# First expert routed alone, gathers in four column groups, and w_out read in eights, in a two-block layer

## The reference

```python
h = h + concat(ssd_out, sc_out) @ w_out            # 2048 -> 1024
hn = rmsnorm(h, norm_ffn)
g_idx = argmax(hn @ w_router_group)                # 4 groups
e_logits = einsum("nd,gde->nge", hn, w_router_expert)   # 8 experts in each
top_v, top_i = top_k(e_logits of the chosen group, 2)
gates = softmax(g_logits)[g_idx] * softmax(top_v)
# each token goes to its two experts:
y = (silu(x @ w_gate[e]) * (x @ w_up[e])) @ w_down[e]   # 1024 -> 512 -> 1024
h = h + sum over the two of gates * y
```

## Time and profile before

| | |
|---|---|
| median of 3 runs | 955.83 us (955.31 to 957.48) |
| the profiled execution | 955.47 us, span 953.7 us |
| TensorE busy | 782.6 us, 82% of the span |
| VectorE busy | 465.6 us, 49% |
| ScalarE busy | 318.0 us, 33% |
| GpSimd busy | 99.0 us, 10% |
| HBM read | 284.85 MB, mean 300 GB/s over the span |
| chain that ended last | TensorE 54%, DMA 28%, issue 8%, VectorE 4%, GpSimd 3%, ScalarE 2% |

### The profile page before, as it was taken

One profiled execution on the slowest core, in us unless ns is written; L12 is line 12 of the kernel. 1 busy time (PEld: TensorE's weight loads), 2 busy tenths in 40 slices (PEclk: granted clock), 3 DMA queues, 4 the chain that ended last, 5 costly groups with the idle time before them and its releaser, 6 DMA issues.

```text
span 953.7 us, 15749 instructions
## 1 busy us (share of the span) xinstructions
PE 782.6 (82%) x6548; PEld 601.2 (63%) x6548; DVE 465.6 (49%) x815; ACT 318.0 (33%) x525; POOL 99.0 (10%) x116
## 2 busy tenths in 40 slices
PE   5999999999984764747646566479999999999997
PEld 5988999777643432334423333236888888888885
DVE  6865849547421121201302012024968776766776
ACT  5764346732100000000000000003597554444444
POOL 3019673300000000000000000000000100000000
PEclk9999999999997887777979798779999999999999
DMA  9895243677999999999999999999975455555101
GB/s 318 272 354 177 90 177 145 259 311 294 415 427 428 426 429 426 427 427 429 428 429 427 428 429 427 429 428 388 363 266 178 155 189 201 183 177 177 45 1 45
DMA packets 72534, 286.67 MB, mean 301 GB/s; under 512 B 11882, under 2 KB 38688, under 8 KB 59936
## 3 DMA queue, kind: packets, MB, share of 16 engines
q1 hardware_dynamic: 71876, 284.81, 75.9%
q10 hardware_dynamic: 604, 1.10, 0.3%
HBM read 284.85 MB, written 1.05 MB: 300 GB/s over the span
## 4 chain that ended last, share of the span: by engine, by line
PE 54%; DMA 28%; issue 8%; DVE 4%; POOL 3%; ACT 2%; SPq 1%; POOLq 0%; DVEq 0%; ACTq 0%
DMA pair_d<-in_w_up_dram 22%; PE bank L664 11%; PE bank L613 11%; PE bank L629 9%; PE bank L2264 5%; PE bank L626 4%; PE bank L2288 4%; PE bank L641 4%; DMA ring<-in_w_in_dram 3%; DMA down_b<-in_w_down_dram 3%; PE bank L2230 1%; PE bank L2238 1%; PE bank L2095 1%; POOL seg_r L946 1%; ACT w_hi L583 1%
## 5 line engine op out<-in xcount | busy, mean ns | idle before, releaser
L593 DVE TENSOR_TENSOR w_lo<-ring,w_hi 128x1024 fp32r<-128x1024 f32 x135 | 174.7, 1294 | 101.9 <-ACT w_hi L583 101.5
L583 ACT ACTIVATE w_hi<-ring 128x1024 fp32r<-128x1024 f32 x136 | 144.2, 1060 | 178.3 <-PE bank L629 64.1
L613 PE MATMUL bank<-act_p,w_hi 128*128 128x256 f32 x736 | 137.7, 288 | 3.1 <-issue 2.0
L1776 DVE COPY y_e<-bank 32x256 f32<-32x256 f32 x64 | 27.2, 424 | 222.5 <-PE bank L2288 222.1
L629 PE MATMUL bank<-act_p,w_hi 128*128 128x512 f32 x344 | 119.3, 397 | 0.0
L613 PEld LDWEIGHTS bank<-act_p,w_hi 128*128 128x128 f32 x736 | 115.3, 192 | 6.0 <-issue 3.9
L1226 ACT ACTIVATE y_e<-bank 32x256 f32<-32x256 f32 x64 | 23.9, 374 | 256.7 <-PE bank L2288 256.4
L613 PE MATMUL bank<-act_p,w_lo 128*128 128x256 f32 x368 | 104.3, 283 | 0.0
L2288 PE MATMUL bank<-down_b,h_t 128*32 128x256 f32 x480 | 40.3, 493 | 74.6 <-issue 64.1
L664 PE MATMUL bank<-w_hi,act_q 128*128 128x512 f32 x288 | 90.6, 396 | 1.4 <-issue 0.8
L2264 PE MATMUL bank<-ring,moe 128*32 128x256 f32 x1472 | 84.0, 380 | 7.1 <-DVE moe L1739 6.7
(11 more groups left out here) (409 smaller groups left out, 1058.5 us busy)
## 6 DMA issues: line engine op xcount, KB each, us to landing
ring<-in_w_up_dram SPq DMA_DIRECT2D x24, 2048.0 KB, 34.6
ring<-in_w_gate_dram SPq DMA_DIRECT2D x23, 2048.0 KB, 30.2
down_a<-in_w_down_dram SPq DMA_DIRECT2D x15, 2048.0 KB, 25.9
down_b<-in_w_down_dram SPq DMA_DIRECT2D x15, 2048.0 KB, 25.8
ring<-in_w_in_dram SPq DMA_DIRECT2D x14, 2048.0 KB, 17.4
ring<-in_w_ffn_in_dram SPq DMA_DIRECT2D x22, 1024.0 KB, 7.6
pair_d<-in_w_gate_dram SPq DMA_DIRECT2D x8, 2048.0 KB, 30.0
pair_d<-in_w_up_dram SPq DMA_DIRECT2D x8, 2048.0 KB, 34.4
```

The lines of the kernel that those rows point to most:

```text
L583: nc.scalar.activation(parts(w_hi, g, view), view, ACT.Copy).then_inc(split_hi, 1)
L593: engine.tensor_tensor(parts(w_lo, g, view), view, h, ALU.subtract).then_inc(split_lo, 1)
L613: mm = nc.tensor.matmul(dst, parts(wt, g, grans[g][1])[:, k, :], a[:, x_part, k, :], start=(k == 0 and i == 0), stop=(k == KC - 1 and i == 2))
L1776: ins = nc.vector.tensor_copy(out_rows(e, j), down_rows(j))
```

## The change

- **w_out in eights.** The granules of w_out are read through a view that puts column c*128 + q where 8q + c was: both splits read words 32 bytes apart, in runs of 128, and write them side by side. The product then has the order of `res`, and `add_res` adds plain halves.
- **Token copy.** GpSimd copies the tokens into `res` after its masks and after granule 0 (`gran_used` 1) and no longer ahead of them.
- **First expert alone.** VectorE first finds only whether a token goes to expert 0: at most one expert of group 0 has a larger logit, and group 0 has the top group logit. Three matmuls of one column give its ranks, and its one-hot follows. The rest of the routing comes behind, with `keep_alone(0)` in its midst; the full ranks (`ranks`) come behind expert 0's gate and up on TensorE.
- **Gathers in column groups.** `gather_alone` takes the one-hot's 32 columns as weights and moves `res` through, 256 features to each of four column groups. The result has slots on partitions; `keep_alone` transposes it in blocks of 32x32 into the tile `gated` and multiplies it with the gain into `x_t`. Experts 0 to 3 have a gather each: 0 ahead of its gate, 1 ahead of its gate, 2 and 3 behind expert 1's gate and up. `gated` is scratch here, and so the combination matrix is built after the fourth.
- **Fillers** are half as wide and stand in more places.

```diff
@@ -225,9 +225,10 @@
-    def row_grans(u, gains):
+    def row_grans(u, gains, eights=False):
         for j, gain in enumerate(gains):
-            grans.append((u, whole(u)[:, j * GR:(j + 1) * GR], gain))
+            view = whole(u)[:, j * GR:(j + 1) * GR]
+            grans.append((u, view.rearrange("p (q c) -> p c q", c=KC) if eights else view, gain))
@@ -250,7 +251,7 @@
         row_grans(rows_unit(w["w_out"], ks[0], 4),
-                  [pcol("sc_norm", k - 8) if k >= 8 else pcol("ssd_norm", k) for k in ks])
+                  [pcol("sc_norm", k - 8) if k >= 8 else pcol("ssd_norm", k) for k in ks], True)
@@ -677,9 +678,9 @@
         for at, (b, half) in enumerate(BY_BLOCK):
-            r = natural(b, 64 * half, 64 * half + 64)
+            r = res[:, b, half * 512:(half + 1) * 512]
             piece_ready(dve, n, at, g)
-            ins = nc.vector.tensor_tensor(r, r, in_eights(banks[2 * b + half][:, :]), ALU.add)
+            ins = nc.vector.tensor_tensor(r, r, banks[2 * b + half][:, :], ALU.add)
@@ -728,6 +729,7 @@
     XT_BANK = 7
+    ALONE_BANK = (6, 5, 6, 5)
@@ -908,8 +910,6 @@
         norm_pool(pool, 0)
-        for b in range(TB):
-            nc.gpsimd.tensor_copy(natural(b), in_eights(x_tok[:, b, :]))
@@ -917,7 +917,11 @@
         nc.gpsimd.affine_select(out=v, in_=v, compare_op=ALU.is_ge, fill=0.0, base=63,
-                                pattern=[[64, 2], [0, 64]], channel_multiplier=-1).then_inc(const_ready, 1)
+                                pattern=[[64, 2], [0, 64]], channel_multiplier=-1)
+        pool.wait_ge(gran_used, 1)
+        for b in range(TB):
+            ins = nc.gpsimd.tensor_copy(natural(b), in_eights(x_tok[:, b, :]))
+        ins.then_inc(const_ready, 1)
@@ -1590,6 +1594,16 @@
+        def keep_alone(e):
+            dve.wait_ge(xt_raw, e + 1)
+            if e:
+                dve.wait_ge(xt_kept, e)
+            turned_rows = gated[:, :, :].rearrange("p b t -> p (b t)")
+            link_dve(dve, nc.vector.transpose(turned_rows, bank[ALONE_BANK[e]][:, 0:2 * P]))
+            nc.vector.tensor_tensor(x_t[:, :, CAP * e:CAP * (e + 1)],
+                                    turned_rows.rearrange("p (c s) -> p c s", c=KC),
+                                    bcast(g_ffn[:, :].unsqueeze(2), [P, KC, CAP]), ALU.mult).then_inc(xt_kept, 1)
@@ -1617,7 +1631,23 @@
         link_dve(dve, ins)
-        nc.vector.tensor_reduce(g_top, by_group(G_LOGIT), AX_X, ALU.max)
+        own = rt[:, 10, :, 0:EPG]
+        nc.vector.tensor_tensor(r8[:, 1, :, :], own, bcast(own[:, :, 0:1], [P, TB, EPG]), ALU.is_gt)
+        link_dve(dve, nc.vector.tensor_reduce(g_top, by_group(G_LOGIT), AX_X, ALU.max))
+        nc.vector.tensor_tensor(r8[:, 2, :, 1], by_group(G_LOGIT)[:, :, 0], g_top, ALU.is_ge)
+        link_dve(dve, nc.vector.tensor_reduce(r8[:, 2, :, 0], r8[:, 1, :, :], AX_X, ALU.add))
+        first = r8[:, 9, :, 2]
+        nc.vector.scalar_tensor_tensor(out=first, in0=r8[:, 2, :, 0], scalar=1.5, in1=r8[:, 2, :, 1], op0=ALU.is_le,
+                                       op1=ALU.mult).then_inc(member, 1)
+        dve.wait_ge(member, 1)
+        dve.wait_ge(rstd_ready, 2)
+        link_dve(dve, nc.vector.tensor_tensor(r8[:, 9, :, 1], first, sm[:, 4:6], ALU.mult))
+        dve.wait_ge(rank_raw, 1)
+        link_dve(dve, nc.vector.tensor_copy(r8[:, 9, :, 0], bank[4][:, 0:TB]))
+        for b in range(TB):
+            ins = nc.vector.tensor_scalar(onehot[:, 1, b, 0:CAP], iota_f[:, 0:CAP], r8[:, 9, b, 0:1], r8[:, 9, b, 1:2],
+                                          ALU.is_equal, ALU.mult)
+        ins.then_inc(member, 1)
@@ -1625,6 +1655,7 @@
                                                      op0=ALU.mult, op1=ALU.add))
+        keep_alone(0)
@@ -1652,15 +1683,7 @@
         link_dve(dve, nc.vector.tensor_scalar(four(10), four(8), float(CAP), None, ALU.mult))
-        dve.wait_ge(rstd_ready, 2)
-        link_dve(dve, nc.vector.tensor_tensor(r8[:, 9, :, 1], rt[:, 4, :, 0], sm[:, 4:6], ALU.mult))
-        dve.wait_ge(rank_raw, 1)
-        first_rank = r8[:, 9, :, 0]
-        link_dve(dve, nc.vector.tensor_copy(first_rank, bank[5][:, 0:TB * NE].rearrange("p (b e) -> p b e", b=TB)[:, :, 0]))
-        for b in range(TB):
-            ins = nc.vector.tensor_scalar(onehot[:, 1, b, 0:CAP], iota_f[:, 0:CAP], r8[:, 9, b, 0:1], r8[:, 9, b, 1:2],
-                                          ALU.is_equal, ALU.mult)
-        ins.then_inc(member, 1)
+        dve.wait_ge(rank_raw, 2)
@@ -1683,7 +1706,7 @@
         def rounds():
-            dve.wait_ge(rank_raw, 2)
+            dve.wait_ge(rank_raw, 3)
@@ -1711,8 +1734,6 @@
             start = isinstance(k, int) and k == 0
-            if start:
-                keep_first(0)
@@ -1720,10 +1741,13 @@
             if start:
-                keep_first(1)
                 gates()
+                keep_alone(1)
                 rounds()
+                keep_alone(2)
+                keep_alone(3)
                 gate_weights()
+                dve.wait_ge(xt_kept, 4)
@@ -1740,24 +1764,7 @@
...
-        def keep_first(half):
...
-        def keep_rest():
...
-        keep_rest()
...
@@ -2037,7 +2044,7 @@
             for _ in range(n):
-                nc.tensor.matmul(bank[4][:, :], ident[:, :], bcast(ident[:, :].unsqueeze(1), [P, 4, P]),
+                nc.tensor.matmul(bank[3][:, 0:2 * P], ident[:, :], bcast(ident[:, :].unsqueeze(1), [P, 2, P]),
@@ -2209,16 +2216,23 @@
             mm.then_inc(logits_raw, 1)
-        keep_running(4)
+        keep_running(3)
         pe.wait_ge(member, 1)
-        nc.tensor.matmul(bank[5][:, 0:NE], m_lt[:, :], rt[:, 4, 0, :], start=True, stop=True)
-        for dst, last in ((bank[5][:, NE:2 * NE], m_lt), (bank[7][:, 0:NE], ones)):
-            nc.tensor.matmul(dst, ones[:, :], rt[:, 4, 0, :], start=True, stop=False)
-            nc.tensor.matmul(dst, last[:, :], rt[:, 4, 1, :], start=False, stop=True).then_inc(rank_raw, 1)
+        first = r8[:, 9, :, 2:3]
+        nc.tensor.matmul(bank[4][:, 0:1], m_lt[:, :], first[:, 0, :], start=True, stop=True)
+        nc.tensor.matmul(bank[4][:, 1:2], ones[:, :], first[:, 0, :], start=True, stop=False)
+        nc.tensor.matmul(bank[4][:, 1:2], m_lt[:, :], first[:, 1, :], start=False, stop=True).then_inc(rank_raw, 1)
+        def ranks():
+            pe.wait_ge(member, 3)
+            nc.tensor.matmul(bank[5][:, 0:NE], m_lt[:, :], rt[:, 4, 0, :], start=True, stop=True)
+            for dst, last in ((bank[5][:, NE:2 * NE], m_lt), (bank[7][:, 0:NE], ones)):
+                nc.tensor.matmul(dst, ones[:, :], rt[:, 4, 0, :], start=True, stop=False)
+                nc.tensor.matmul(dst, last[:, :], rt[:, 4, 1, :], start=False, stop=True).then_inc(rank_raw, 1)
@@ -2231,22 +2245,23 @@
-        def gather_first(o, n, banks, which):
-            for c in range(KC):
-                for b in range(TB):
-                    mm = nc.tensor.matmul(banks[c // 4][:, (c % 4) * n:(c % 4 + 1) * n], tokens(b, c),
-                                          onehot[:, which, b, o:o + n], start=(b == 0), stop=(b == TB - 1))
-                if c % 4 == 3:
-                    mm.then_inc(xt_raw, 1)
+        def gather_alone(e, which, o):
+            for b in range(TB):
+                row = res[:, b, :].rearrange("t (c p) -> t c p", c=KC)
+                for j in range(4):
+                    mm = nc.tensor.matmul(bank[ALONE_BANK[e]][CAP * j:CAP * (j + 1), 0:2 * P],
+                                          onehot[:, which, b, o:o + CAP], row[:, :, CAP * j:CAP * (j + 1)],
+                                          start=(b == 0), stop=(b == TB - 1))
+            mm.then_inc(xt_raw, 1)
                 for c in range(KC):
-                    if c % 4 == 0:
-                        pe.wait_ge(xt_kept, c // 4 + 1)
+                    if c == 0:
+                        pe.wait_ge(xt_kept, 1)
@@ -2325,18 +2340,29 @@
             else:
+                gather_alone(0, 1, 0)
+                keep_running(2)
                 gate_up_apart(0)
+                keep_running(1)
+                ranks()
+                keep_running(6)
                 pe.wait_ge(built, 2)
-                gather_first(CAP, P - CAP, bank[5:7], 0)
+                gather_alone(1, 0, CAP)
+                keep_running(2)
+                pe.wait_ge(xt_kept, 2)
+                gate_up_pe(k, 1)
+                for e in range(2, 4):
+                    gather_alone(e, 0, CAP * e)
             mm.then_inc(gmat_raw, 1)
-            if before is None:
+            if before is not None:
+                gate_up_pe(k, 1)
+            else:
                 pe.wait_ge(xt_kept, 4)
-            gate_up_pe(k, 1)
@@ -2350,7 +2376,6 @@
         pe.wait_ge(member, 2)
-        gather_first(0, CAP, (bank[6], bank[1]), 1)
```

More of the change, by code:

```diff
@@ L1741, in keep_xt @@
                 bcast(g_ffn[:, 4 * half:4 * half + 4].unsqueeze(2), [P, 4, P]), ALU.mult).then_inc(xt_kept, 1)
-        def keep_first(half):
-            dve.wait_ge(xt_raw, half + 1)
```

(13 more changed lines are left out.)

## The result

| | before | changed |
|---|---|---|
| median | 956.22 us (955.31 to 957.48, 4 runs) | 971.04 us (970.14 to 971.76, 4 runs) |
| profiled execution | 955.47 us, span 953.7 | 970.14 us, span 968.4 |

The changed kernel is slower by 1.54% (ratio 1.0154, 95% interval 1.0136 to 1.0171), 14.8 us by the medians and 14.7 by the profiled executions. Forecast was 3.6 us slower with 963 us as the upper end. The sign was right, the size was not, and 4.0 us of it arise in a stretch that the prediction had not touched.

What follows compares the result with a forecast made beforehand. It took the queue of expert weights to bound the kernel, with the routing's hole and the w_out splits ahead of it. 955.47 - 0.9 - 3.7 + 0 + 8.2 = 959.1 us; forecast's own range 955 to 963, over all cases 950 to 963.

Steps and rivals of the forecast that it cites:

- Reads in eights (+8.2): Output projection: splits reading w_out at a stride of 8 words cost VectorE 0.82 and ScalarE 0.41 us, 8.2 us lost.
- the prediction's count of places: Output projection: both engines' extra time reaches the path at six granules, ScalarE's share alone at two more.
- The rule that the prediction cites from the Trainium skill: SBUF reads: 16-byte lines, each crossing to a new line pays, on ScalarE as well; total near 962 us.
- Rival "reads are free": Output projection: reads in eights cost nothing and the projection keeps its pace, 950.9 us; chance 0.31.
- Adds (-0.9): End of the projection: contiguous adds take 0.688 us for 1.056, so block 1's transposes start earlier, 0.9 us gained.
- First expert alone (-5.7, then +2.0): Routing: expert 0's gate starts 5.7 us earlier, 2.0 given back before expert 1, 3.7 us gained.
- Rival "the clock falls": Behind the routing: TensorE's clock drops and one of two gates runs slow, about 3.5 us lost, 962.6 us; chance 0.06.
- Token copy (0): GpSimd's token copy, moved behind granule 0: taken as 0, ends 1.3 us gained to 1 lost.
- The fourth gather costs nothing: First experts: combination matrix waits for it, expert 2's issue moves from 250.5 to 252.3 us, queue not empty, no cost.
- The hole in the weights' rate: Weight stream around the routing: the hole shrinks to about 3 us, from 7.5.
- A microsecond by which that stream is refilled earlier should reach the end.: Weight stream of the 32 experts: its queue is never empty, so every earlier refill shortens the whole kernel equally.
- The sign that the prediction had named for it: Stream's end moving otherwise than the start of expert 5's gate transfer would show the queue claim wrong.

Runs made afterwards that it cites:

- hi_alone: Kernel before, with only ScalarE's split (high part) reading w_out in eights: 964.51 us, ratio 1.0084.
- lo_alone: Kernel before, with only VectorE's split (low part) reading w_out in eights, and plain adds: 961.53 us, ratio 1.0056.
- no_eights: Changed kernel with w_out read side by side again and the scattered adds back: 957.28 us, ratio 1.001.
- before_52: Kernel before plus 52 instructions of waits for what has long come, at the head of TensorE's program: 964.06 us, ratio 1.0080.
- before_hid36: Kernel before plus 36 instructions of waits behind the first products of w_out: 959.23 us, ratio 1.0026.
- wide_fill: no_eights with eight fillers of 512 columns for sixteen of 256, 32 instructions fewer: 954.47 us, ratio 0.9976.
- point 7: Changed kernel with w_out side by side and 204 waits at TensorE's head, token copy moved back to its old place: 974.44 us against 974.55 without that move.
- before_hid52: Kernel before plus 52 instructions of waits behind the first products of w_out: 960.06 us, ratio 1.0030.
- after_hid: Changed kernel as it is, plus 204 waits behind the products of w_out: 973.14 us, ratio 1.0167.
- no_eights_hid: no_eights plus 204 waits behind the products of w_out: 955.63 us, ratio 0.9981.

## Why the prediction was wrong

- **Reads in eights (+8.2).** The step that failed is the term "taken 0.41" for ScalarE, between 0 and 0.82. It measured 1.13 us (2.28 for 1.15), outside its own range. The upper end had been taken from VectorE's extra time, on the idea that ScalarE could not lose more. But ScalarE's operation, whose one large operand is the scattered one, took 2.0 times as long, and VectorE's, which reads a second one side by side, 1.6 to 1.7 times; that the second operand makes the difference is likely, not shown. VectorE's 0.82 was right, 0.8 to 0.9. With 1.13 in the prediction's count of places, six times 0.82 + 1.13 and twice 1.13, the sum is 14.0, what was measured. That it fits to a tenth is partly luck. By the same count `hi_alone` should lose 9.0 and lost 8.2, `lo_alone` 4.9 and lost 6.3; and in the changed kernel the stretch from the first split to that of granule 50 grew by 3.8 us for 5.0 counted, the rest up to the adds by 10.2 for 8.9.
- **The rule that the prediction cites from the Trainium skill** ("SBUF — State Buffer", Specifications (TRN2)), with both engines at their upper end, gave 962, about 8 us short. Of that 2.5 is ScalarE's price, taken there from the same row of VectorE; 4.0 is the loop and 1.5 the clock, which this rule does not touch.
- **Rival "reads are free".** Wrong, and for the reason stated against it: step 4 costs what step 128 does.
- **Adds (-0.9).** Right: first add to first reduction went from 8.9 to 7.9 us, 1.0.
- **First expert alone (-5.7, then +2.0).** Right where the clock held (`no_eights`: 5.6 and 3.6 net, expert 1 starting 6.4 us after expert 0 ends, as forecast). The prediction's own terms add up to 4.7 and 6.3 where it wrote 4.8 and 6.4. In the changed kernel the lower clock took 1.5 us of it (6.3 us from reduction to gate, for 4.74).
- **Rival "the clock falls".** It came, ahead of expert 0 instead of in a gate, and cost 1.5, not 3.5. With at least one of the two splits reading apart it came behind the adds and by the end of expert 0's gate in all six profiles, with side-by-side splits in three of ten (`before_52`, `before_hid36`, `wide_fill`), and in `before_52` it hit the gate itself, as the rival had it (5.32 us for 3.70): `before_hid36`, which has the fillers and the routing of the kernel before, shows 0.50 from 222 to 226 us, where the kernel before shows 1.00. So the fillers alone do not decide it; that the longer waits of the projection favour it is likely but not shown.
- **Token copy (0).** Its worth is not shown (point 7). Locally both sides were as described: transposes at 9.57 us (forecast 9.6), and a low part of 2.02 us at 17.44.
- **The fourth gather costs nothing.** The issue behind expert 2 comes 13.1 us after that behind expert 1, forecast 11.6; the rest is expert 0's down at the lower clock (3.22 us for 1.9). The queue did not run empty there (401 to 426 GB/s from 258 to 268 us), as said.
- **The hole in the weights' rate.** Forecast about 3 us, measured 2.6 + 1.9 = 4.5, with the lower clock in it.
- **"A microsecond by which that stream is refilled earlier should reach the end."** This is the second step that failed, and no term stood for it. The sign that the prediction had named for it came: the start of expert 5's transfer moved by 10.4 us, the last of the landings above by 15.2. In its place the runs show that loads of instructions, which depend on the place of the loop, slow the stream: by 2.4 and 2.6 us in the medians of `before_hid36` and `before_hid52`, by 4.0 in the changed kernel's trace.

The sum with what was measured: 955.5 + 14.0 - 1.0 - 3.6 + 1.5 = 966.4, and 4.0 in the loop makes 970.4, against 970.14. The 4.0 is read from two traces, and the test that should have taken it away again on the changed kernel, `after_hid`, missed; the scatter of the first split, 162.6 to 165.3 us, is larger than what the sum leaves over.

## What to carry to other kernels

A rearranged view is not free because the instruction stays the same: four bytes read 16 or more bytes apart took 1.6 to 2 times as long on ScalarE and VectorE, and 1.9 times on TensorE at the one step tried, so bound such a price by twice the operation and not by another engine's difference. Put the scattered side where few operations pay for it: four adds that each lost 0.37 us were traded here for 32 splits that each lose 0.8 to 1.1 us. And where a long loop streams weights, look at the queue of instructions inside it: a few dozen instructions more ahead of the loop cost here as much as a good edit ahead of it gained.

## What the hardware showed that I had not expected

- Reads of 4-byte words: 1.15, 1.22, 2.12 us for steps of 1, 2 and 4 words on ScalarE, 1.28, 1.29, 2.07 on VectorE, and within 0.2 us of the last up to 128 words. TensorE's moving operand, at 8 words: 0.43 us per 128x512 pass for 0.23.
- A loop whose place in the program makes its instructions come again in every pass, some nine packets of 16 KB in 117 us, and four experts' weights then take up to 60.3 us for 58.7 (68.01 MB of weights in 160 us for 68.59).
- Waits for semaphores that have long come are not free: 204 instructions of them took 22 us with nothing else in hand, and 0.8 us between the products of w_out (51.65 us from split to add in `no_eights_hid` for 50.8 to 50.9).
